# GpSimd's S5 phase tables made in fewer blocks, two pieces to a block, in a two-layer hybrid trunk

## The reference

```python
for layer in range(DEPTH):
    u = _rmsnorm(h, norm_g[layer])
    (gq, gk, gv, ga, g_gate, s_in, s_gate, aq, ak, av, a_gate, m_gate) = _split_in(u @ w_in[layer])
    y_gla = (_gla_mixer(gq, gk, gv, ga, ...) * silu(g_gate)) @ w_gla_out[layer]
    y_s5 = (_s5_mixer(s_in, s5_a_re[layer], s5_a_im[layer], ...) * silu(s_gate)) @ w_s5_out[layer]
    y_att = (_swa_mixer(aq, ak, av, ...) * silu(a_gate)) @ w_attn_out[layer]
    gates = sigmoid(m_gate).reshape(B, L, N_BRANCH, D_MODEL)
    mix = gates[:, :, 0] * y_gla + gates[:, :, 1] * y_s5 + gates[:, :, 2] * y_att
    h = h + mix @ w_out[layer]
return _rmsnorm(h, final_norm_g)[:, N_META:]
```

## Time and profile before

| | us |
|---|---|
| median of 3 runs | 1894.04 |
| lowest and highest run | 1890.87, 1894.38 |
| span of the profiled execution | 1894.7 |
| busy in the span: TensorE, VectorE, ScalarE, GpSimd | 1747.2, 927.3, 701.2, 788.6 |

### The profile page before, as it was taken

The page is one execution under the profiler, slowest core; times in us unless marked ns, Lnnn a source line. Parts: engine busy times, 40 slices in busy tenths (PEclk is TensorE's granted clock), DMA queues, the critical chain, the costliest instruction groups (busy, mean ns, idle before and its releaser), DMA issues.

```text
span 1894.7 us, 31165 instructions
## 1 busy us (share of the span) xinstructions
PE 1747.2 (92%) x12985; PEld 1538.7 (81%) x12985; DVE 927.3 (49%) x1471; ACT 701.2 (37%) x1332; POOL 788.6 (42%) x490
## 2 busy tenths in 40 slices
PE   5967899999998999988997999999999898999997
PEld 4967798999887889987897987777788676788885
DVE  7985134333438992374453222533334598624223
ACT  3453442444543113332233543334455322224322
POOL 1655575333232223332343685653332332344442
PEclk8988999999999999998898999999999998999999
DMA  8543244322375653535342433542223956433432
GB/s 146 149 108 105 72 115 118 85 67 72 92 153 131 158 146 107 112 82 149 87 124 55 133 90 90 113 118 78 67 75 101 169 156 155 124 100 92 143 104 85
DMA packets 363539, 209.56 MB, mean 111 GB/s; under 512 B 75524, under 2 KB 350136, under 8 KB 360840
## 3 DMA queue, kind: packets, MB, share of 16 engines
q1 hardware_dynamic: 350600, 187.92, 38.7%
q10 hardware_dynamic: 12800, 19.66, 3.5%
HBM read 170.34 MB, written 36.67 MB: 109 GB/s over the span
## 4 chain that ended last, share of the span: by engine, by line
PE 68%; DVE 10%; POOL 7%; DMA 5%; ACT 5%; issue 3%; SPq 2%; ACTq 1%; DVEq 0%; POOLq 0%
PE ring L844 52%; DMA sb_w_raw<-in_w_in 4%; POOL sb_w_lo L686 3%; PE ring L803 3%; DVE sb_s_prod L1631 2%; PE ring L825 2%; PE aux L1115 1%; SPq L580 1%; PE aux L1224 1%; PE aux L1160 1%; PE aux L1136 1%; DMA s_matrices<-sb_s_phase 1%; DVE sb_s_rot L2136 1%; DVE sb_s_rot L1631 1%; PE aux L1163 1%
## 5 line engine op out<-in xcount | busy, mean ns | idle before, releaser
L686 POOL TENSOR_TENSOR sb_w_lo<-sb_w_raw,sb_w_hi 128x1024 fp32r<-128x1024 f32 x246 | 609.0, 2477 | 1026.3 <-ACT sb_w_hi L1275 1023.9
L1275 ACT ACTIVATE sb_w_hi<-sb_w_raw 128x1024 fp32r<-128x1024 f32 x246 | 260.0, 1057 | 602.7 <-DMA sb_w_raw<-in_w_in 398.7
L844 PE MATMUL ring<-sb_u_hi,sb_w_hi 128*128 128x264 f32 (+1 forms) x2112 | 368.5, 329 | 24.6 <-DVE sb_tmp_dve L1711 14.6
L844 PEld LDWEIGHTS ring<-sb_u_hi,sb_w_hi 128*128 128x128 f32 x2112 | 314.3, 203 | 63.3 <-DVE sb_tmp_dve L1711 16.5
L844 PE MATMUL ring<-sb_u_lo,sb_w_hi 128*128 128x264 f32 (+1 forms) x2112 | 340.8, 312 | 0.0
L844 PE MATMUL ring<-sb_u_hi,sb_w_lo 128*128 128x264 f32 (+1 forms) x2112 | 334.6, 309 | 0.0
L844 PEld LDWEIGHTS ring<-sb_u_lo,sb_w_hi 128*128 128x128 f32 x2112 | 300.6, 192 | 22.0
L844 PEld LDWEIGHTS ring<-sb_u_hi,sb_w_lo 128*128 128x128 f32 x2112 | 294.1, 188 | 21.0
L1307 ACT ACTIVATE sb_tmp_act<-ring 128x528 f32<-128x528 f32 (+1 forms) x112 | 67.3, 601 | 138.6 <-PE ring L844 135.8
L1746 DVE SCALAR_TENSOR_TENSOR sb_tmp_dve<-sb_tmp_act,ring 128x528 f32<-128x528 f32 (+1 forms) x32 | 22.3, 696 | 142.0 <-PE ring L844 130.0
L1551 ACT ACTIVATE sb_att_scores<-sb_att_scores,sb_att_neg_max 128x208 f32<-128x208 f32 x128 | 58.5, 458 | 82.7 <-DVE sb_att_neg_max L1929 82.7
(11 more groups left out here) (333 smaller groups left out, 2455.7 us busy)
## 6 DMA issues: line engine op xcount, KB each, us to landing
sb_w_raw<-in_w_in SPq DMA_DIRECT2D x166, 512.0 KB, 4.1
sb_s_loaded<-s_matrices ACTq DMA_DIRECT2D x16, 1040.0 KB
s_matrices<-sb_s_phase SPq DMA_DIRECT2D x16, 528.0 KB, 3.1
sb_w_raw<-in_w_gla_out SPq DMA_DIRECT2D x16, 512.0 KB, 3.5
sb_w_raw<-in_w_attn_out SPq DMA_DIRECT2D x16, 512.0 KB, 3.5
sb_w_raw<-in_s_w_glu SPq DMA_DIRECT2D x16, 512.0 KB, 3.5
sb_w_raw<-in_w_s_out SPq DMA_DIRECT2D x16, 512.0 KB, 3.5
sb_w_raw<-in_w_out SPq DMA_DIRECT2D x16, 512.0 KB, 3.5
```

The source lines that it names most:

```text
L686: pool.tensor_tensor(WL[:, w], WR[:, w], WH[:, w].bitcast(F32), ALU.subtract).then_inc(lo_ready, 1)
L844: last = pe.matmul(RING[:, 2 * r + hf, 0:c1 - c0], w[:, n % SLOTS, kt, :], moving(b[0], xx[:, kt], c0, c1), start=(term == 0 and kt == 0), ...
L1275: act.activation(WH[:, w], WR[:, w], ACT.Copy).then_inc(hi_ready, 1)
```

## The change

In layer 0 the pieces start at block gq1 (14) and not at gv0 (5), and there are two behind each low part. In layer 1 they stay at one per block from gv0. The turn in which SyncE issues the spill of set j is worked out anew: in layer 0 it was 14+2j and is now 19+j; in layer 1 it was 14+2j and is now 15+2j.

```diff
-PHASE_FIRST = BLOCKS.index(("gv", 0))
+PHASE_FIRST = (BLOCKS.index(("gq", 1)), BLOCKS.index(("gv", 0)))
+PHASE_STEPS = (2, 1)
 PHASE_BASE = 9
-PHASE_SPILL = {BLOCKS[PHASE_FIRST + PHASE_BASE + 2 * j]: j for j in range(KT)}
+PHASE_SPILL = {(ly, BLOCKS[PHASE_FIRST[ly] + (PHASE_BASE + 2 * j + 1) // PHASE_STEPS[ly]]): j
+               for ly in range(2) for j in range(KT)}
...
-                    if name in PHASE_SPILL:
-                        spill_phase(ly, PHASE_SPILL[name])
+                    if (ly, name) in PHASE_SPILL:
+                        spill_phase(ly, PHASE_SPILL[ly, name])
...
-                    if b >= PHASE_FIRST:
-                        next(work, None)
+                    if b >= PHASE_FIRST[ly]:
+                        for _ in range(PHASE_STEPS[ly]):
+                            next(work, None)
```

## The result

The changed kernel takes 1913.45 us (median of 4 runs, 1908.36 to 1920.03); the kernel before, timed beside it, 1894.21 us. The ratio is 1.0088, 95% interval 1.0052 to 1.0124: slower by 19 us going by the medians, by 17 us (10 to 23) going by the ratio. The forecast was 1914 us.

A forecast was written before the change was run, and what follows sets the result against it. GpSimd's turn of 12.85 us, with its wait for the spill, was taken to bound layer 0. Span 1894.7 + 20.2 (layer 0) + 0 (layer 1) = 1914.9, median 0.7 below the span: 1914 us, range 1904 to 1921.

The forecast's parts named there:

- What binds: Layer 0 from block 19: GpSimd's turn becomes the bound, TensorE waiting about 5 us a block.
- Part 1: Layer 0, pieces leave blocks 5 to 13: shorter TensorE wait before 174.17 us, gain 4.5 us, bounds 0 and 6.2.
- the rival of the locked ports: Layer 0, blocks 5 to 13: small pieces cost VectorE as much as large ones, gain 0, total 1918.5 us; chance 0.13.
- Start of the chain: Layer 0: spill 0 waits behind block 21's load; 3.1 us to land, piece a of set 1 starts at 225.9 us.
- The turn: Layer 0, from block 19: GpSimd's lo, b, wait for the spill and a take 12.85 us, against TensorE's block of 7.87.
- Behind the chain: Layer 0 behind block 26: old idles of 1.0 and 3.2 us and 1.5 of low clock go, -5.7 us.
- Layer 0 in all: Layer 0's sum: 24.4 + 1.5 - 5.7 = +20.2 us, with the 4.5 us gain at blocks 5 to 13 inside it.
- The bias window: SyncE's turn 25: bias issues of 13.5 us (layer 0) and 13.95 (layer 1) delay a spill; idles some 8 and 6 us.
- Layer 1, predicted 0: Layer 1, spills one turn later: transposes 1.7 us sooner, block 27 +4.2, old idle mostly goes; value 0, bounds -2 and +3.
- The milder queue: Layer 0: post-spill instructions start without the full 3.2 us, or spill 0 precedes load 21; 10 us less, 1904; chance 0.09.
- SyncE freed: Spills stop holding weight loads; if GpSimd's turn fits under TensorE's block, limit 7.9 us, layer 0 gains, 1884; chance 0.06.

The follow-up runs named there:

- The pause at blocks 14 and 15: The kernel before, with no layer 0 pieces in blocks 14 and 15, two each in 16 and 17, spill 0 in turn 15; 1895.46 us, ratio 1.0025.
- the run with the early signal alone: The kernel before, with GpSimd signalling a finished set right behind piece b, not behind the next low part, in both layers; 1874.77 us, ratio 0.9888.

## Why the prediction was right, step by step

**What binds.** Right, and shown: GpSimd's serial turn in layer 0. Without the wait for the spill in it the same pieces give 1876 us; with a turn of some 10.5 in place of 12.7 us and the same late start, 1896 us.

**Part 1, predicted -4.5, measured -6.5.** The size was low. Ahead of the last matrices TensorE idles 1.40 us (171.06) and not 5.55, and its next block runs at 2.18 us, not 3.87. The pause at blocks 14 and 15, which touches nothing else there, gives 6.6; both lie just beyond the upper bound of 6.2. VectorE's and GpSimd's timelines of the changed kernel show why the small pieces cost VectorE less than I took:

```profile
156.62 2.40 DVE L2108 TENSOR_SCALAR sb_s_skip_diag<-sb_eye_by_group,sb_params 128x16 f32<-128x16 f32 x1
...
160.50 1.26 DVE L1779 TENSOR_TENSOR_SCAN sb_gla_decay<-sb_chunk_reset,sb_tmp_dve 128x528 f32<-128x528 f32 x1
...
167.55 3.08 DVE L1634 TENSOR_TENSOR sb_s_mb<-sb_s_mat_prod 128x256 f32<-128x256 f32 x2
```

```profile
156.23 2.60 POOL L688 TENSOR_TENSOR sb_w_lo<-sb_w_raw,sb_w_hi 128x1024 fp32r<-128x1024 f32 x1 [10.69 <-ACT sb_w_hi L1278]
...
159.33 1.25 POOL L727 COPY sb_s_phase_ones<-sb_s_a 128x32 f32<-128x32 f32 x2
160.66 1.15 POOL L700 TENSOR_TENSOR sb_s_phase_tmp<-sb_s_phase_ones 128x32 f32<-128x32 f32 x1
...
180.44 0.24 POOL L700 TENSOR_TENSOR sb_s_phase_tmp<-sb_s_phase_twelves 128x32 f32<-128x32 f32 x1
```

The scan at 160.50 takes 1.26 us, as a free one. The one that waited was GpSimd: its product at 160.66 took 1.15 us, until the scan had ended, and the one of the same shape at 180.44 took 0.24. Beside a low part it is VectorE that stands: the narrow operation at 156.62 took 2.40 us, the pair at 167.55 took 3.08 where the pair just before 156.62 took 0.76 together. So the rival of the locked ports (1918.5) fell, though not the lock: the one that stands waits for what is left of one instruction of the other, and a small piece has little left. Four products of VectorE beside small pieces took 1.90 us (at 165.62), where they take 1.43 free and took 3.33 beside large ones. The scan of 1.40 us, on which I rested, was no proof against the lock: GpSimd's 128x128 product beside it, at 136.25, took 1.29 us, and one of the same shape at 134.06 took 0.39. The rule that I cited from the Trainium skill (SBUF — State Buffer, the shared port pair) agrees with these rows; my reading of it, that small pieces block as well as large ones, was the error in that rival.

**Start of the chain, predicted spill 0 at 222.8 and a of set 1 at 225.9.** The spill left at 221.98, a started at 227.50: 5.5 us, not 3.1. It leaves right behind a weight load (221.57). The later ones of layer 0 took 3.0 to 3.1 us, and 3.4 behind the bias window. No run was made for the cause, but the traces agree on it: the 15 spills of whole sets that left 0.4 to 0.5 us behind a weight load landed after 5.4 to 6.9 us, the 12 with no other transfer in flight after 2.7, and most of those with a load right behind them after 3.0 to 3.3. My 3.1 us came from spills of the last kind.

**The turn, predicted 12.85 us, measured 12.7** (231.12 to 294.50 for five). Low part 26 was done at 309.62 + 2.34 = 312.0, predicted 310.4. The idle was predicted as 5 us a block and is 3.0 to 4.4: the other 1.1 to 1.6 us of the turn's excess over 7.87 us are the slow last thirds (3.68 at 246.24 for 2.10). As long as GpSimd sets the pace, TensorE's lower clock costs nothing; it only fills the wait (low parts 12.6 to 12.7 us apart, whether the last third took 2.22 or 3.68 us). Behind the chain: predicted -5.7, measured -5.0 (shift +26.9 to +21.9). Layer 0 in all: predicted +20.2, measured +21.9.

**The bias window.** Place and idle were right (8 us predicted, 7.47 measured), the part of the window in it was not: the run with the spill ahead of it shows that GpSimd's own turn would have held the spill nearly as long in layer 0. In layer 1 the window does cost what was said: GpSimd waited 14.90 us, TensorE 5.36 us (predicted 6), a step of 5.5 us (predicted 4.2).

**Layer 1, predicted 0 (-2 to +3).** Measured between -2 and -8 us in the traces and nothing in the medians. The transposes come sooner as predicted (idle 1.47 and 1.39 for 3.11). What I had wrong is the end: low part 29 is not 2.3 us late and no idle follows. And I counted only one of the three old idles behind block 27, the 1.55 us at 1256.04; the 1.94 and 2.24 us ahead of it go too, with the slow matmuls behind them.

**The other rivals.** The milder queue (1904) did not come: waits of 3.2 us stand in full. SyncE freed (1884) did not come in this form, because the turn was 12.7 and not under 7.9 us. But the kernel with no wait shows that the limit of 7.9 us was too strict: 9.6 us a turn were hidden by the head start, and the gain I named there was real (1876). I had the signal's place in front of me and used it only to add up a turn: that the spill leaves behind the low part and not behind b is in the earlier trace rows (b 268.14, low part 271.78, wait 3.20), and it cost the kernel before 20 us (the run with the early signal alone).

**Where the signs came from.** Layer 0's +22 minus layer 1's few us is 14 to 20; the medians say 19. The errors also offset each other: the first landing was 2.4 us longer than I had it, layer 1 gave back more. The agreement of 1914 and 1913.45 to half a microsecond is luck within a scatter of 10.

## What to carry to other kernels

A buffer that is filled, sent off and filled again is a ring: fill, signal, transfer, refill. Add up the ring and compare it with the pace of what is behind it before packing its steps closer; then look where in it the signal is given, because work that stands between the last write and the signal is paid in every round (here one moved line, 20 us). A gain that comes from moving work away can be lost again, as half of it was here in the run with the pause, where a transfer that it moves stands in front of others in the same queue.

## What the runs showed of the hardware

- Contention of VectorE and GpSimd falls on either side: a 1.26 us scan kept its time while GpSimd's 128x32 product went from 0.24 to 1.15 us; a 128x16 operation of VectorE took 2.40 us beside a low part of 2.60.
- TensorE ran its last thirds at 3.2 to 3.9 us in place of 2.1 after idles of 3 us and more, but the one at 271.55, also after an idle of 2.99 us, took 2.22. And the same 16 matmuls for the chunk states near 213 to 220 us, behind the same idle of 2.92 us, took 2.00 us in seven of the twelve traces and 3.55 to 3.68 in five.
- A spill of 528 KB landed 2.7 us after its issue with no other transfer in flight, and after 5.4 to 6.9 us when issued 0.4 to 0.5 us behind a 512 KB load of the same queue.
- The same code between 608 and 1100 us differs by 1 to 9 us from one profiled execution to the next, and runs of one kernel by up to 0.7% to either side.
